# Attention stage of a decoder step on one core: where one block of maxima, the head loads and the page groups stand in a hand-written order

## The chip, the cores and the metric

The kernel runs on one core of one Trainium2 chip. The metric is device microseconds of a whole execution, the median of a few runs. The kernel before took 3463.64 us (three runs, 3452.68 to 3472.67). The core has a matrix engine (PE, TensorE; its weight loads are listed as PEld), a vector engine (DVE), a scalar engine (ACT), a general engine (POOL) and a sequencer that here only issues transfers (SP). Each works through its own instructions in program order and waits on semaphores for the others.

## The reference, cut to what matters

The program is one inference step of a two-layer decoder for a prompt of 2048 tokens and 8 samples of one token each. The change touches only the attention of layer 1, over 16 heads of 64 features:

```python
# prompt: every head, causal, with a cumulative forget bias ck
s = einsum('bqhd,bkhd->bhqk', q_i, k) * ATTN_SCALE + cq_i[..., :, None] - ck[:, :, None, :]
p = softmax(where(key_pos <= q_pos, s, -inf));  out = einsum('bhqk,bkhd->bqhd', p, v)
# samples: 8 of them, each over 32 cached pages of 128 rows (4096 keys) and its new row
past_v = cache_v[page_table].reshape(Bs, -1, C_HEADS, C_HEAD_DIM)
s = einsum('bqhd,bkhd->bhqk', q, k_all) * ATTN_SCALE + cq[..., :, None] - ck[:, :, None, :]
out = einsum('bhqk,bkhd->bqhd', softmax(where(mask, s, -inf)), v_all)
```

Everything is float32; the softmax needs the maximum of each query's row, or any value near it.

## The kernel before

The attention stage is one function, `attention`. The prompt's work is cut into units: unit u is head u // 4 and a block of 512 queries, u % 4. A unit has 4, 8, 12 or 16 *score steps*, one for each 128 keys that its queries may see, so a head has 40 steps and the stage 640. In the last four steps of a unit (the diagonal) the width shrinks from 512 queries to 384, 256 and 128, and a 128-wide matmul adds the causal mask.

A step n is, in the names of `schedule()`:

- QK: two matmuls into one of two PSUM tiles `at_st` (L2052, L2054, and the mask L2056). PE waits until the exponential of step n-2 is done. ACT then takes the exponential into one of six tiles `at_w` (L2121), and POOL adds it to the row sums `at_acc` (L1995).
- M: one block of maxima for a later unit. A matmul into one of two tiles `at_mx` (L2030, mask L2033), which DVE reduces (L2153). The two tiles are a ring: PE waits for the reduction of the block two before. When a unit's last block is reduced, MN takes its maximum (L2159), MR turns it into a row with four small matmuls (L2040), and ACT writes it as an extra row of the queries (L2138).
- PV: for every pair of steps, two matmuls of values with weights, side by side on the two halves of the array (L2069). OE and OF (ACT L2128, DVE L2168 and L2171) add the halves of a finished unit and apply the gate.
- LS: once for each head, the row sums (L2077), which are stored by L1874.

There are 640 blocks of maxima as well. Twelve are made before step 0. After that the number in a step is set by `pace`, which divides the blocks owed by the steps left, for units up to u+2: two a step in the first eight steps of a head, one a step in the next twenty-four, none in the last eight.

The sample attention is threaded through this. Each of the 8 samples gets 80 steps, two heads. Its ten small operations are SD, SM, SA, SB, SC, SS, SE, SL, SX and SR: decayed scores, their maximum over pages and partitions, exponential, sum, inverse. They go from DVE (SD, SM, SB, SS, SL, SR) to PE (SA, SC, SX) and ACT (SE) and back, each waiting for the one before. Then come eight page groups (VG 0 to 7, 16 matmul records each at L2101), the new row (VN), VM (DVE), VA (PE) and VC (DVE). `side` spreads these 22 evenly, one every 3.6 steps: SD at step 3, SR at 36, VG 0 at 39, then 43, 47, 50, 54, 58, 61 and 65, VN at 69.

All transfers are issued by SP in the order of the same list. A page group is four transfers of 512 KB into one of two buffers `at_vp` (L1878, function `values`); group r+2 is asked for when group r is used up. A head needs eight loads (LD, L1856), seven of them 512 KB, and its values (LV, L1861). LV fetches 2048 rows of 256 bytes. In `schedule` LD x of head h+1 stands at step 2+x of head h (for h from 1), and LV at step 10. Head 0 and head 1 are loaded before the first step; PE's first block of maxima waits for all eight loads of its head.

## Time and profile before

| what | value |
|---|---|
| median of three runs | 3463.64 us (3452.68 to 3472.67) |
| the profiled execution, its own time | 3444.23 us |
| its span, first to last instruction | 3442.6 us |
| mean granted clock of PE over the span | 0.927 of 2.4 GHz |
| first and last block of maxima's matmul in the attention stage (L2030) | 1956.7 and 3166.4 us |
| first and last score exponential (L2121) | 1970.8 and 3196.6 us |

The chain that ended last names only the last stage (`o_...`), 7% of the span, so it doesn't tell of attention. The stage must be read from its own windows. A stage in which PE is busy nearly all the time and idles in a few long gaps has its time in PE's work, in PE's clock and in those gaps. The window view gives, for each stretch, the busy time of each engine with its number of instructions, the granted clock of PE as a share of full speed, the busy share of the 16 DMA engines and their rate.

### The profile page before, as it was taken

What the parts mean: (1) busy time and instruction counts of PE and PEld (TensorE: products, weight loads), DVE (VectorE), ACT (ScalarE), POOL (GpSimd) and SP (SyncE); (2) the same over time, 40 slices, a digit from 0 to 9 for tenths busy, and PEclk for the clock granted to TensorE, in tenths of its full rate; (3) what the DMA queues carried; (4) which work ended last, traced back from release to release, by engine and by line L of the source; (5) the groups of instructions that cost most, each with busy time, mean ns of one, the idle gap of its engine ahead of it and who ended that gap; (6) DMA issues with size and microseconds to landing.
All of it is one profiled execution on the core that took longest, in us unless ns stands there. A gap on an engine that the chain in (4) does not pass through costs nothing. (4 is left out here: it accounts for less than half of the span.)

```text
span 3442.6 us, 46928 instructions
## 1 busy us (share of the span) xinstructions
PE 2965.1 (86%) x17133; PEld 2233.3 (65%) x17133; DVE 1591.6 (46%) x2148; ACT 1028.9 (30%) x1721; POOL 1377.1 (40%) x986
## 2 busy tenths in 40 slices
PE   3869797959889998889999398887989898899899
PEld 3869696947659998789999244443535344444687
DVE  5142323243556788865554453443435353444332
ACT  5222222231452221211121043433434343434200
POOL 0000000010003777678888264554657464556100
PEclk9989898979999999999999598998999898999899
DMA  3101010026545888788776557566574857664442
GB/s 114 32 23 41 32 37 25 24 83 182 170 144 170 268 278 273 250 288 255 245 254 223 138 148 219 143 188 178 143 208 126 248 136 217 156 193 161 151 129 69
DMA packets 327904, 547.51 MB, mean 159 GB/s; under 512 B 76093, under 2 KB 220129, under 8 KB 319212
## 3 DMA queue, kind: packets, MB, share of 16 engines
q1 hardware_dynamic: 263564, 471.12, 46.9%
q10 hardware_dynamic: 61120, 58.83, 4.9%
q0 software_dynamic: 3008, 14.81, 1.2%
q8 instruction: 124, 2.03, 0.2%
q14 instruction: 88, 0.72, 0.1%
HBM read 449.58 MB, written 95.12 MB: 158 GB/s over the span
## 5 line engine op out<-in xcount | busy, mean ns | idle before, releaser
L1995 POOL TENSOR_TENSOR at_acc<-at_acc,at_w 128x512 f32<-128x512 f32 (+3 forms) x576 | 640.1, 1111 | 420.1 <-ACT at_w L2121 370.6
L1151 POOL TENSOR_TENSOR p_kp<-p_kp,p_qb 128x1024 f32<-128x1024 f32 x256 | 628.6, 2484 | 388.8 <-DMA p_kp<-in_cache_k_dram 307.8
L2153 DVE TENSOR_REDUCE at_mx<-at_mx 128x1 f32<-128x512 f32 (+3 forms) x640 | 377.0, 608 | 642.4 <-PE at_mx L2030 369.9
L112 PE MATMUL p_pb<-p_w,x_xh 128*128 128x256 f32 x2048 | 592.3, 289 | 9.3 <-DVE p_w L1465 9.3
L2121 ACT ACTIVATE at_w<-at_st,c_nckt 128x512 f32<-128x512 f32 (+3 forms) x640 | 393.5, 623 | 672.1 <-PE at_st L2054 426.0
L113 PE MATMUL p_pb<-p_w,x_xh 128*128 128x256 f32 x2048 | 579.6, 283 | 0.0
L114 PE MATMUL p_pb<-p_w,x_xl 128*128 128x256 f32 x2048 | 579.3, 283 | 0.0
L1567 DVE TENSOR_REDUCE p_sc<-p_kp 128x16 f32<-128x1024 f32 x256 | 307.7, 1215 | 225.4 <-POOL p_kp L1151 225.3
L112 PEld LDWEIGHTS p_pb<-p_w,x_xh 128*128 128x128 f32 x2048 | 391.2, 191 | 21.6 <-issue 11.4
L113 PEld LDWEIGHTS p_pb<-p_w,x_xh 128*128 128x128 f32 x2048 | 392.5, 192 | 0.0
L114 PEld LDWEIGHTS p_pb<-p_w,x_xl 128*128 128x128 f32 x2048 | 391.8, 191 | 0.0
L112 PE MATMUL l_pb<-x_xh,l_wh 128*128 128x412 f32 x800 | 288.9, 361 | 73.5 <-DVE l_wl L857 73.5
L2069 PE MATMUL at_o<-at_w,at_v 128*64 128x512 f32 (+3 forms) x1280 | 335.3, 582 | 0.0
L2052 PEld LDWEIGHTS at_st<-at_q,at_k 128*128 128x128 f32 x640 | 125.3, 196 | 302.0 <-issue 148.4
L2030 PE MATMUL at_mx<-at_km,at_q 65*128 65x512 f32 (+3 forms) x640 | 253.8, 419 | 46.0 <-DMA at_k<-kl 22.1
L2052 PE MATMUL at_st<-at_q,at_k 128*128 128x512 f32 (+3 forms) x640 | 289.9, 453 | 0.0
L113 PE MATMUL l_pb<-x_xl,l_wh 128*128 128x412 f32 x800 | 286.1, 358 | 0.0
L114 PE MATMUL l_pb<-x_xh,l_wl 128*128 128x412 f32 x800 | 285.7, 357 | 0.0
L112 PE MATMUL o_pp<-o_wh,o_mh 128*128 128x512 f32 (+1 forms) x544 | 219.7, 404 | 36.8 <-DVE o_wl L586 22.4
L2101 PE MATMUL at_cv<-at_vp,at_sw 128*32 128x512 f32 x1056 | 164.1, 704 | 95.6 <-DMA at_vp<-in_cache_v_dram 95.6
L2054 PE MATMUL at_st<-at_q,at_k 65*128 65x512 f32 (+3 forms) x640 | 243.0, 380 | 0.0
L113 PE MATMUL o_pp<-o_wl,o_mh 128*128 128x512 f32 (+1 forms) x544 | 214.8, 395 | 0.0
(293 smaller groups left out, 3897.4 us busy)
## 6 DMA issues: line engine op xcount, KB each, us to landing
p_kp<-in_cache_k_dram SPq DMA_DIRECT2D x256, 512.0 KB, 4.8
at_vp<-in_cache_v_dram SPq DMA_DIRECT2D x256, 512.0 KB, 5.6
o_mt<-mixed SPq DMA_DIRECT2D x32, 512.0 KB, 5.6
p_raw<-in_w_in_dram SPq DMA_DIRECT2D x32, 512.0 KB, 7.0
at_q<-qh SPq DMA_DIRECT2D x32, 512.0 KB
at_k<-kh SPq DMA_DIRECT2D x32, 512.0 KB
l_raw<-in_w_in_dram SPq DMA_DIRECT2D x20, 512.0 KB
mixed<-l_w POOLq DMA_DIRECT2D x8, 1028.0 KB, 4.2
```

The costliest lines, as they stand in the source:

```text
L112: nc.tensor.matmul(out, lhs[0], rhs[0], start=(k == 0), stop=False)
L113: nc.tensor.matmul(out, lhs[0], rhs[1], start=False, stop=False)
L114: return nc.tensor.matmul(out, lhs[1], rhs[0], start=False, stop=(k == nk - 1))
L1151: nc.gpsimd.tensor_tensor(kp[:, g % 4], kp[:, g % 4], qb[:], ALU.mult).then_inc(kmul, 1)
L1567: nc.vector.tensor_reduce(sc[:, b % 2].rearrange("p (h g) -> p h g", g=z.PG)[:, :, r], by_head(kp[:, g % 4], z.H), AX.X, ALU.add).then_inc ...
L1995: nc.gpsimd.tensor_tensor(t[:, 512 - wd:512], t[:, 512 - wd:512], W[n % RW][:, 0:wd], ALU.add).then_inc(accd, 1)
L2030: last = nc.tensor.matmul(MX[r % 2][:, 0:wd], Q2[s][0:HR, t * P:(t + 1) * P], KM[s][0:HR, seg * 512:seg * 512 + wd], start=True, stop=seg < c)
L2052: nc.tensor.matmul(ST[n % 2][:, 0:wd], K1[s][:, ks], Q1[s][:, q0:q0 + wd], start=True, stop=False)
L2054: last = nc.tensor.matmul(ST[n % 2][:, 0:wd], K2[s][:, ks], Q2[s][:, q0:q0 + wd], start=False, stop=not diagonal)
L2069: last = nc.tensor.matmul(O[u % 2][HD * x:HD * x + HD, 512 - wd:512], V[s][:, kb + x, :], W[(n + x) % RW][:, 0:wd], start=kb == 0, stop=kb ...
L2121: nc.scalar.activation(W[n % RW][:, 0:wd], ST[n % 2][:, 0:wd], ACT.Exp, bias=C.nckt[:, kb, u // NC:u // NC + 1]).then_inc(ex, 1)
L2153: nc.vector.reduce_max(mx[:, u % 2, j, seg:seg + 1], MX[r % 2][:, 0:wd], AX.X).then_inc(mread, 1)
```

## The change

It sets the order by other rules, and gives the steps these places (counted from the start of a head for LD and LV, of a sample for the rest):

- M: up to two a step as long as fewer than n + 21 are done. In the first head that gives two a step for eight steps; after that it is exactly one in every step until all are done, 21 steps before the end.
- The ten small sample operations stand at steps 1 to 10, one a step. VG r stands at step 13 + 8r (13 to 69), VN at 71, VM 72, VA 74, VC 76.
- LD 0 to 7 stand at steps 2, 4, 4, 8, 14, 18, 22 and 26, LV at 11. Head 1 is loaded in the same way and no longer before the first step. A second semaphore (`ldm`) counts the three loads that the maxima need; the other five are waited for by the head's first score step.
- LS stands three steps earlier. There are six tiles `at_acc`, in turn by unit, in place of eight.
- PV is written so that it could take other than even pairs. With the pairs that the list has, its matmuls are the same as before.

```diff
@@ -1679,6 +1679,8 @@
     NLD = 8
     VG = PG // 4
     RW = 6
+    LEAD = 20
+    NA = 6
 
     def blocks(u):
         return 4 * (u % NC + 1)
@@ -1700,13 +1702,18 @@
         todo = [(v, j, seg) for v in range(U) for j in range(4) for seg in range(v % NC + 1)]
         tail = [("SD",), ("SM",), ("SA",), ("SB",), ("SC",), ("SS",), ("SE",), ("SL",), ("SX",), ("SR",)] \
             + [("VG", r) for r in range(VG)] + [("VN",), ("VM",), ("VA",), ("VC",)]
-        side = [(*w, b) for b in range(B) for w in tail]
+        at = [1 + x for x in range(len(tail) - VG - 4)] + [13 + 8 * r for r in range(VG)] + [71, 72, 74, 76]
+        span = N // B
+        side = {}
+        for b in range(B):
+            for w, x in zip(tail, at):
+                side.setdefault(span * b + x, []).append((*w, b))
         loads = {}
-        for h in range(2, H):
-            start = first_step(NC * (h - 1)) + 2
-            for x in range(NLD):
-                loads.setdefault(start + x, []).append(("LD", h, x))
-            loads.setdefault(start + NLD, []).append(("LV", h))
+        for h in range(1, H):
+            start = first_step(NC * (h - 1))
+            for x, later in enumerate((2, 4, 4, 8, 14, 18, 22, 26)):
+                loads.setdefault(start + later, []).append(("LD", h, x))
+            loads.setdefault(start + 11, []).append(("LV", h))
         later = {}
         seq, done, ring, turn_at, pending = [], 0, 0, {}, []
 
@@ -1752,14 +1759,7 @@
                     else:
                         seq.append(w)
                 seq.append(("QK", u, kb, n))
-                pace = 0
-                for v in range(u + 1, min(u + 3, U)):
-                    owed = sum(blocks(x) for x in range(0, v + 1)) - done
-                    left = first_step(v) - 4 - n
-                    pace = max(pace, -(-owed // left) if left > 0 else owed)
-                for _ in range(pace):
-                    if done == len(todo) or todo[done][0] > u + 2:
-                        break
+                for _ in range(min(2, min(len(todo), n + 1 + LEAD) - done)):
                     v = maximum()
                     if v is not None:
                         turn_at.setdefault(n + 2, []).append(v)
@@ -1771,9 +1771,8 @@
                     if p[1] == blocks(p[0]) - 2:
                         later.setdefault(n + 2, []).append(("OF", p[0]))
                         if p[0] % NC == NC - 1:
-                            later.setdefault(n + 8, []).append(("LS", p[0] // NC))
-                a0, a1 = (len(side) * n) // N, (len(side) * (n + 1)) // N
-                seq += side[a0:a1]
+                            later.setdefault(n + 5, []).append(("LS", p[0] // NC))
+                seq += side.pop(n, [])
                 n += 1
         for n in sorted(later):
             seq += later[n]
@@ -1781,7 +1780,7 @@
             weigh(p)
         seq.append(("OF", U - 1))
         sums(H - 1)
-        assert n == N and done == len(todo) and not turn_at and not loads
+        assert n == N and done == len(todo) and not turn_at and not loads and not side
         return seq
 
     SEQ = schedule()
@@ -1797,7 +1796,7 @@
         V = [S.sb(f"v_{s}", [P, z.NT, HD]) for s in range(2)]
         SG = [S.sb(f"sg_{s}", [HD, 512]) for s in range(2)]
         W = [S.sb(f"w_{x}", [P, 512]) for x in range(RW)]
-        acc = [S.sb(f"acc_{x}", [P, 512]) for x in range(2 * NC)]
+        acc = [S.sb(f"acc_{x}", [P, 512]) for x in range(NA)]
         ot = [S.sb(f"ot_{x}", [HD, 512]) for x in range(2)]
         og = [S.sb(f"og_{x}", [HD, 512]) for x in range(2)]
         lt = S.sb("lt", [P, 512])
@@ -1836,6 +1835,7 @@
             "table_in vnew_in scores_in new_scores_in new_scores_zeroed decayed smax sall ssub sexp ssum sl4 slsum srcp vpages vmasked"
             " vatt vcopied made masked sgs_in final fstored sl1 rl_bounded masks_rounded sdiag sspread smhd")
         ld = S.sems("head_in0 head_in1")
+        ldm = S.sems("head_for_max0 head_for_max1")
         sg_in = S.sems("gate_in0 gate_in1")
         val_in = S.sems("values_in0 values_in1")
         ogst = S.sems("out_stored0 out_stored1")
@@ -1853,7 +1853,7 @@
                 dst, src = ((Q2[s][0:HD], D.qh[hs, :]), (KM[s][0:HD], D.kh[hs, :]), (KM[s][HD:HR], D.nck[ds(h, 1), :]),
                             (K1[s][0:HD], D.kh[hs, :]), (K1[s][HD:P], D.kh[hs, :]), (Q1[s][0:HD], D.qh[hs, :]),
                             (Q1[s][HD:P], D.ql[hs, :]), (K2[s][0:HD], D.kl[hs, :]))[x]
-                sp.dma_start(dst.bitcast(F32), src).then_inc(ld[s], 16)
+                sp.dma_start(dst.bitcast(F32), src).then_inc((ldm if x < 3 else ld)[s], 16)
 
             def value_load(h):
                 if h >= 2:
@@ -1903,12 +1903,9 @@
             scores(0)
             sp.wait_ge(snz, 1)
             sp.dma_start(sn[0:1], D.snew.rearrange("(o b) h -> o b h", o=1)).then_inc(sn_in, 16)
-            for x in range(NLD):
-                head_load(1, x)
             sp.wait_ge(pt_in, 16)
             value_group(0, 0)
             value_group(0, 1)
-            value_load(1)
             for b in range(B):
                 sp.dma_start(sgs[:, :, b], D.sgs[b].rearrange("(k p) -> p k", p=P)).then_inc(sgs_in, 16)
             due = []
@@ -1984,17 +1981,17 @@
                     _, u, kb, n = w
                     h, c = u // NC, u % NC
                     wd = width(n)
-                    t = acc[NC * (h % 2) + c]
+                    t = acc[u % NA]
                     pool.wait_ge(ex, n + 1)
                     if kb == 0:
-                        if h >= 2:
-                            pool.wait_ge(lsm, h - 1)
+                        if u >= NA:
+                            pool.wait_ge(lsm, (u - NA) // NC + 1)
                         nc.gpsimd.tensor_copy(t[:], W[n % RW][:]).then_inc(accd, 1)
                     else:
                         pool.wait_ge(accd, n)
                         nc.gpsimd.tensor_tensor(t[:, 512 - wd:512], t[:, 512 - wd:512], W[n % RW][:, 0:wd], ALU.add).then_inc(accd, 1)
                     added = n + 1
-                elif w[0] == "LD" and w[2] == 0:
+                elif w[0] == "LD" and w[2] == 0 and w[1] >= 2:
                     h = w[1]
                     pool.wait_ge(qk, first_step(NC * (h - 1)))
                     pool.wait_ge(accd, added)
@@ -2022,7 +2019,7 @@
                     c, h = u % NC, u // NC
                     s = h % 2
                     if j == 0 and seg == 0 and c == 0:
-                        pe.wait_ge(ld[s], 16 * NLD * (h // 2 + 1))
+                        pe.wait_ge(ldm[s], 16 * 3 * (h // 2 + 1))
                         pe.wait_ge(onesd, max(2, h + 1))
                     ring_free(r)
                     t = 4 * c + j
@@ -2048,6 +2045,8 @@
                         pe.wait_ge(ex, n - 1)
                     if kb == 0:
                         pe.wait_ge(rowd, u + 1)
+                        if c == 0:
+                            pe.wait_ge(ld[s], 16 * (NLD - 3) * (u // NC // 2 + 1))
                     ks = slice(kb * P, (kb + 1) * P)
                     nc.tensor.matmul(ST[n % 2][:, 0:wd], K1[s][:, ks], Q1[s][:, q0:q0 + wd], start=True, stop=False)
                     diagonal = kb >= 4 * c
@@ -2065,16 +2064,16 @@
                     if kb == 0 and u >= 2:
                         pe.wait_ge(osum, u - 1)
                     for x in range(2):
-                        wd = width(n + x)
-                        last = nc.tensor.matmul(O[u % 2][HD * x:HD * x + HD, 512 - wd:512], V[s][:, kb + x, :], W[(n + x) % RW][:, 0:wd],
-                                                start=kb == 0, stop=kb == blocks(u) - 2)
+                        wd, y = width(n + x), HD * (x % 2)
+                        last = nc.tensor.matmul(O[u % 2][y:y + HD, 512 - wd:512], V[s][:, kb + x, :], W[(n + x) % RW][:, 0:wd],
+                                                start=kb + x < 2, stop=kb + x >= blocks(u) - 2)
                     last.then_inc(pv, 1)
                 elif w[0] == "LS":
                     _, h, r = w
                     pe.wait_ge(accd, HB * (h + 1))
                     ring_free(r)
                     for c in range(NC):
-                        last = nc.tensor.matmul(MX[r % 2][32 * c:32 * c + 32, :], ones32[:], acc[NC * (h % 2) + c][:], start=True, stop=True)
+                        last = nc.tensor.matmul(MX[r % 2][32 * c:32 * c + 32, :], ones32[:], acc[(NC * h + c) % NA][:], start=True, stop=True)
                     last.then_inc(lsm, 1)
                 elif w[0] == "SA":
                     pe.wait_ge(smaxd, w[-1] + 1)
```

PE, at the last steps of head 0 and the first of head 1, before (`at_st` are scores, `at_mx` on the left is a block of maxima, `at_o` values with weights, `at_cv<-at_vp` a page group):

```order
L2052 MATMUL at_st<-at_q_0,at_k_0 128x512
L2054 MATMUL at_st<-at_q_0,at_k_0 128x512
L2052 MATMUL at_st<-at_q_0,at_k_0 128x512
L2054 MATMUL at_st<-at_q_0,at_k_0 128x512
L2069 MATMUL at_o<-at_w,at_v 64x512 x2
...
L2101 MATMUL at_cv<-at_vp,at_sw 32x512 x8
L2052 MATMUL at_st<-at_q_1,at_k_1 128x512
L2054 MATMUL at_st<-at_q_1,at_k_1 128x512
L2056 MATMUL at_st<-at_identr,at_maskr 128x128
L2030 MATMUL at_mx<-at_km,at_q_1 128x512 x2
```

The same place now:

```order
L2051 MATMUL at_st<-at_q_0,at_k_0 128x512
L2053 MATMUL at_st<-at_q_0,at_k_0 128x512
L2027 MATMUL at_mx<-at_km,at_q_1 128x128
L2030 MATMUL at_mx<-at_maskr,at_identr 128x128
L2051 MATMUL at_st<-at_q_0,at_k_0 128x512
L2053 MATMUL at_st<-at_q_0,at_k_0 128x512
L2027 MATMUL at_mx<-at_km,at_q_1 128x512
L2068 MATMUL at_o<-at_w,at_v 64x512 x2
...
L2051 MATMUL at_st<-at_q_1,at_k_1 128x512
L2053 MATMUL at_st<-at_q_1,at_k_1 128x512
L2055 MATMUL at_st<-at_identr,at_maskr 128x128
L2027 MATMUL at_mx<-at_km,at_q_1 128x384
```

Steps 34 and 35 had no block of maxima and now have one each; step 40, the first of the next head, had two and now has one; and the page group at the head's last step is gone from there.

SP, at the loads of head 2 in the middle of sample 0, before (`at_q_0`, `at_km`, `at_k_0` are the head's loads, `at_v` its values, `at_vp` pages, `lsum` the store of the sums):

```order
L1856 DMA at_km<-nck 1x2048
L1870 DMA att<-at_og 64x512
L1865 DMA at_sg<-sg 64x512
L1856 DMA at_k_0<-kh 64x2048 x2
L1856 DMA at_q_0<-qh 64x2048
...
L1856 DMA at_q_0<-ql 64x2048
L1870 DMA att<-at_og 64x512
L1865 DMA at_sg<-sg 64x512
L1856 DMA at_k_0<-kl 64x2048
L1861 DMA at_v<-out_v_prompt_dram 128x16x64
L1874 DMA lsum<-at_lt 4x512
```

The same loads now:

```order
L1874 DMA lsum<-at_lt 4x512
L1856 DMA at_k_0<-kh 64x2048
L1870 DMA att<-at_og 64x512
L1865 DMA at_sg<-sg 64x512
L1861 DMA at_v<-out_v_prompt_dram 128x16x64
...
L1856 DMA at_k_0<-kh 64x2048
L1870 DMA att<-at_og 64x512
L1865 DMA at_sg<-sg 64x512
L1856 DMA at_q_0<-qh 64x2048
```

The store of the sums, which stood right behind the values' load, stands ahead of it, and a page group (the rows left out, four transfers) and two units' stores now stand between loads that were issued one after the other.

## Rows read from the trace of the kernel before

**Rows 1.** The page: the span.

```profile
span 3442.6 us, 46928 instructions
```

**Rows 2.** What PE waited for, 1950 to 3200 us: total, times, longest.

```profile
PE at_cv L2101 <- DMA at_vp<-in_cache_v_dram: 95.6, 17, 11.0
...
PE at_mx L2030 <- DVE at_mx L2153: 19.8, 46, 1.3
```

**Rows 3.** Windows, one for each sample's 80 steps (first, last, sum of eight).

```profile
core 0: us, PE busy (x) PEld busy (x) DVE busy (x) ACT busy (x) POOL busy (x), PEclk, DMA share, GB/s
1970.83:2126.58 155.75, 139.15 (x652) 70.46 (x652) 65.03 (x116) 59.55 (x97) 86.54 (x81) 0.88 0.67 189
...
3064.36:3196.99 132.63, 128.45 (x633) 62.40 (x633) 59.38 (x104) 58.90 (x97) 85.27 (x80) 0.96 0.49 142
sum 1226.16, PE 1098.01 PEld 539.48 DVE 524.62 ACT 483.10 POOL 703.15; mean PE 137.25 PEld 67.43 DVE 65.58 ACT 60.39 POOL 87.89
```

**Rows 4.** Windows of sample 5: steps 0-12, 12-24, 24-32, 32-40, 40-52, 52-64, 64-72, 72-80.

```profile
2756.96:2778.50 21.54, 19.93 (x95) 10.51 (x95) 15.46 (x29) 9.24 (x17) 12.97 (x14) 1.00 0.78 175
2778.50:2796.14 17.64, 16.37 (x77) 8.96 (x76) 11.13 (x19) 8.80 (x15) 13.27 (x12) 1.00 0.43 80
2796.14:2806.68 10.54, 10.54 (x51) 6.07 (x50) 8.12 (x13) 7.64 (x12) 7.37 (x7) 1.00 0.13 26
2806.68:2817.47 10.79, 10.79 (x59) 4.84 (x58) 0.32 (x2) 5.12 (x9) 9.79 (x8) 1.00 0.00 0
2817.47:2844.03 26.56, 25.25 (x142) 11.80 (x142) 14.29 (x26) 9.23 (x16) 14.17 (x16) 1.00 0.96 264
2844.03:2881.57 37.54, 25.82 (x123) 10.82 (x122) 9.31 (x16) 8.80 (x15) 12.98 (x12) 0.77 0.93 284
2881.57:2895.82 14.25, 14.25 (x70) 6.62 (x69) 7.13 (x12) 6.68 (x11) 8.99 (x8) 1.00 0.55 179
2895.82:2909.48 13.66, 13.66 (x58) 7.34 (x56) 0.58 (x2) 5.34 (x9) 9.33 (x9) 0.75 0.53 181
```

**Rows 5.** Windows of the last sample: steps 52-64 and 72-80.

```profile
3154.43:3174.88 20.45, 20.45 (x115) 8.93 (x114) 7.20 (x11) 8.69 (x15) 13.03 (x12) 1.00 0.96 334
...
3186.67:3196.99 10.32, 10.32 (x49) 5.64 (x48) 0.17 (x1) 4.54 (x8) 8.82 (x8) 0.83 0.01 2
```

**Rows 6.** Windows of steps 52-64, samples 0 to 6: their sum.

```profile
sum 272.40, PE 182.32 PEld 76.19 DVE 65.15 ACT 61.57 POOL 90.77; mean PE 26.05 PEld 10.88 DVE 9.31 ACT 8.80 POOL 12.97
```

**Rows 7.** Timeline of SP in sample 5: start, duration, instruction.

```profile
2842.10 0.59 SPq L1861 DMA_DIRECT2D at_v<-out_v_prompt_dram  x1
2842.74 14.54 SPq L1874 DMA_DIRECT2D lsum<-at_lt  x1
```

**Rows 8.** Timeline of PE in sample 5, page group 4.

```profile
2853.84 3.64 PE L2101 MATMUL at_cv<-at_vp,at_sw 128*32 128x512 f32 x16 [7.43 <-DMA at_vp<-in_cache_v_dram]
```

**Rows 9.** Windows, the last sample's steps 52-64, page matmuls alone.

```profile
3154.43:3174.88 20.45, 5.77 (x48) 1.25 (x48) 1.00 0.96 334
```

**Rows 10.** Groups by form, 1950 to 3200 us: DVE, ACT and POOL.

```profile
L2153 DVE TENSOR_REDUCE at_mx<-at_mx 128x1 f32<-128x512 f32 x448 | 302.8, 688 | 444.7 <-PE at_mx L2030 369.9 <-PE at_mx L2033 72.1
...
L2194 DVE TENSOR_REDUCE at_l<-at_sw 128x32 f32<-128x1056 f32 x8 | 16.5, 2065 | 0.0
...
L2141 ACT ACTIVATE at_sw<-at_sd 128x528 f32<-128x528 f32 x8 | 9.3, 1166 | 0.0
...
L1995 POOL TENSOR_TENSOR at_acc<-at_acc,at_w 128x512 f32<-128x512 f32 x384 | 496.0, 1292 | 336.0 <-ACT at_w L2121 304.0
```

**Rows 11.** Timeline of the stage's beginning: POOL, PE.

```profile
1946.30 0.34 POOL L1970 MEMSET at_onesh<- 16x128 f32 x1
...
1956.65 0.44 PE L2030 MATMUL at_mx<-at_km,at_q 65*128 65x128 f32 x1 [22.05 <-DMA at_k<-kl]
...
1968.55 0.77 PE L2052 MATMUL at_st<-at_q,at_k 128*128 128x512 f32 x1
```

## The prediction

> **What bounds the kernel now.** I read the page first: its chain covers the last 7% of the span alone, so attention has to be read from windows. The waits of PE over the stage come next [rows 2]. One wait stands out: 95.6 us in 17 waits, up to 11.0 us long, for a page group from memory. Waits for DVE's reductions of the maxima, the ring of two tiles, add up to only 19.8 us. The windows per sample [rows 3] show PE busy for 1098.01 of 1226.16 us while DVE, ACT and POOL are each busy for 703 us or less: PE sets the pace, by its work, its clock and its gaps. The first and the last sample, and what the sum leaves for the rest, show the next thing. The last takes 132.63 us and the other seven (1226.16 - 132.63) / 7 = 156.2 us each, with nearly the same work. The last is the one with no further head to load. It also lacks the final 20 blocks of maxima, which I price below.
>
> The windows within one sample say where the difference is. Steps 52 to 64 take 37.54 us in sample 5 at a clock of 0.77 [rows 4], 272.40 / 7 = 38.9 us on average [rows 6], and 20.45 us at full clock in the last [rows 5], with the same three page groups. So it is not the page traffic alone that is late there: the last sample draws its pages at 334 GB/s without a wait. It is the head's loads, all at steps 42 to 50 between page groups 1 and 4. SP's own timeline shows how this hurts [rows 7]: after the values' load it is held for 14.54 us at issuing the next transfer, 8 KB of row sums, and what stands behind it, the request for page group 5, goes out only after that. PE waits 7.43 us for group 4 and then takes 3.64 us for it [rows 8]; in the last sample a group costs 5.77 / 3 = 1.92 us [rows 9]. That is the other half of the loss: after the gap PE runs at 1.2 instead of 2.4 GHz for a while.
>
> Meanwhile steps 24 to 40 of the same sample move next to nothing, 26 and 0 GB/s [rows 4]. The memory traffic is bunched; it isn't too much.
>
> **Term 1, the page groups spread (VG every 8 steps, loads spread too).** After the change a group comes every 8 steps and is asked for 16 steps ahead. At the 1.3 to 1.5 us a step of the undisturbed windows (10.54 / 8, 17.64 / 12, [rows 4]) plus a quarter microsecond a step for the groups, 16 steps are about 25 us. Demand: a sample draws 176 GB/s or so over some 155 us, the 173 to 189 of its windows, so about 28 MB (189 x 155.75 = 29.4 MB in the first [rows 3], the last, with fewer loads, 142 x 132.63 = 18.8 MB). In 130 us that is 215 GB/s, against 334 GB/s that the queue has shown [rows 5] and 264 to 284 while it was crowded [rows 4]. So I take the waits to be gone, and the clock with them. Price: steps 52 to 64 fall from 38.9 to the last sample's 20.45 plus four blocks of maxima that it lacked, at 0.25 us, 21.5 us: 17.4 us in each of seven samples, 122 us. A few samples also lose some time in steps 44 to 52, which I put at 9 us together. Term 1: -131 us. If nothing is gained (the wait only moves), it is 0; more than the whole difference to the last sample, 7 x (156.2 - 132.6) = 165 us, it can't be.
>
> The groups themselves cost the same wherever they stand, 1.92 us each. VN, VM, VA and VC also only move.
>
> **Term 2, one block of maxima a step.** It moves eight blocks per head, from its first eight steps to the last eight of the head before. Before, steps 0 to 12 took 21.54 us [rows 4] with DVE busy 15.46 us, and steps 40 to 52 took 26.56, from which three groups (5.8) and LS (about 1) come off: 19.8. What do twelve such steps cost with one block each? The nearest row is steps 52 to 64 of the last sample without its groups, 20.45 - 5.8 = 14.7 us, with wider scores but only eight blocks; I take 15. That saves 6.5 and 4.8 us, 5.65 a head. On the other side the last eight steps of a head get eight blocks. Full-width steps with a block take 10.54 / 8 = 1.32 us; without one, and with a group, narrower steps take 10.79 [rows 4], 8.9 without the group, 1.1 each. So a block costs about 0.25 us, 2 us for eight. Head 0 stays as it was and gets only the extra; the last gets only the saving: 15 x 5.65 - 15 x 2 = 55 us. Term 2: -55 us; bounds -20 (if DVE was no part of it, and only PE's order changes) and -85 (if the added blocks hide in PE's waits for ACT).
>
> **Term 3, the ten small operations one a step.** This is what gets worse. PE takes three of them in order (SA, SC, SX) and stands still until DVE or ACT has delivered. In steps 1 to 10 DVE now has two units' OF, ten or eleven reductions of at most 0.69 us, and all of the sample's work, of which the sum over the weights alone is 2.07 us, and ACT's exponential of 1.17 us [rows 10] comes before that. SX at step 9 waits for both in a row: 3.2 us and the copy behind them, against two steps of PE. I price it at +3.5 us a sample, less about 1 us that such a stall cost before in steps 12 to 24 (17.64 us there [rows 4] against the 15.7 of rows 5 without groups, but with the blocks it lacked). Term 3: 8 x 2.5 = +20 us. Bounds: 0 and, if all of the chain were exposed (about 9 us a sample), +72 us. Behind a waiting SX stand the next scores, and behind these ACT and POOL; POOL's adds at 1.29 us each have room in a 1.5 us step, so nobody else becomes late.
>
> **Term 4, the clock outside of steps 40 to 64.** Steps 72 to 80 without any block took 13.66 us at a clock of 0.75 in sample 5, and 10.32 at 0.83 in the last [rows 4, 5]. With blocks in them PE is busier. I take 2 us a sample, -15 us in all; bounds 0 and -30.
>
> **Term 5, the beginning.** PE's first block stood until 1956.65 for the last of eight loads [rows 11]. It now waits for the first three. PE's other condition, constants of POOL, is met at 1946.6 [rows 11]. The first twelve blocks and two MR take 1956.65 to 1968.55, 11.9 us, and can now run before the other loads land. Score step 0 starts at about 1958.6: -10 us, bounds 0 and -12.
>
> LS three steps earlier: it has waited for POOL for almost nothing, and I price it at 0, at worst 1 us a head, +16. Six sum tiles instead of eight: the first that is reused is unit 6's, at step 52, long after LS. PV: no change.
>
> **The sum.** -131 - 55 + 20 - 15 - 10 = -191 us. The span of 3442.6 us [rows 1] becomes about 3252, and that execution's 3444 about 3253. It was a quick one: the median of the runs is 3464. Taking the same difference from the median gives 3273; I say 3270. As a check, eight samples of 80 steps by the windows at full clock: 15 + 3.5, then 15.7 + 3.8 (two groups), 10.5 + 1.9, 8.9 + 2 + 1.9, 15 + 1 + 1.9, 15.7 + 3.8, 14.2, and 10.3 + 2 make 127 us, 1016 in all, against 1226: -210, of which the first sample's slow beginning (about 13 us, two blocks a step at half clock) and some slow stretches come back.
>
> At one place a rule speaks against it. The values' load moves 2048 pieces of 256 bytes, and the row shows SP held for 14.54 us right behind it [rows 7]. The Trainium skill, DMA: Bandwidth & Descriptors, Specifications, says the same from the other side: below 512 B per piece a transfer doesn't reach the line rate. By that rule the load stays as costly as it was, and it now stands at step 11, two steps ahead of a page request.
>
> **Rivals.** A, the transfers stay late in part. For: the change puts the values' load at steps 11 and 51 of a sample, just ahead of the requests at VG 0 and VG 5, so SP may be held there twice. Against: the groups then asked for are needed 16 steps later, 25 us, more than the 14.54. If half of term 1 stays, -125 us: 3340.
>
> B, slower: the same mechanism at its full price. If SP is held behind both values' loads long enough that groups 2 and 7 land late, each place costs PE what one place costs now, 17.4 us a sample, in all 14 to 16 places: 15 x 17.4 = 261 us, against 131 now, so term 1 turns into +130, and with the others +70: 3534. It decides from about 25 us between request and landing; a hold of 14.54 plus a group in 8 leaves it just short. The rule above would have it, if small pieces were what fills the queue.
>
> C, the chain of small operations is exposed in full and PE's clock falls there as it did behind the page groups: term 3 at +72 and term 4 at 0, -124 us: 3340.
>
> D, the change does not do what it says: SP runs ahead of PE, so the spread exists only where SP waits (VG, stores). Then loads bunch again, between other groups. That is A's price. And the maxima are only moved for 8 of 40 steps, which term 2 already counts.
>
> **How the numbers follow.** The forecast has 0.70, A with D 0.13, C 0.12, B 0.04, and 0.01 for nothing measurable. Its own range is 3215 to 3310; over the cases, 3205 to 3345. A run-to-run difference of about 0.5% (17 us) is what can be told from no change: faster 0.95, same 0.01, slower 0.04.
>
> **What will show it.** In the profile after: PE's wait for page groups near 0 instead of 95.6 us; no window of 12 steps over 24 us after the first sample; the clock in steps 52 to 64 at 1.0; DMA at 150 GB/s or more in steps 24 to 40. The seven samples are at 127 to 131 us. In steps 0 to 12, 17 to 19 us, with short waits of PE for DVE at SA, SC and SX. PE's first block at 1947 and score step 0 at about 1959. It would be wrong if a page wait of several us stood behind step 29 or 69 (B), or if steps 0 to 12 took over 22 us (C).

## The result and the profile after

The changed kernel took 3315.81 us (median of four runs, 3305.91 to 3319.65) against 3468.15 us for the kernel before: a ratio of 0.9546, 95% interval 0.9475 to 0.9616. That is 4.5% less, 152 us by the medians. Between the two profiled executions it is 3442.6 - 3304.3 = 138 us of span. The forecast was 191 us. The time lies 6 us above the forecast's own range (3215 to 3310), and within the one over all its cases (3205 to 3345).

The page of the changed kernel, the span:

```profile
span 3304.3 us, 46930 instructions
```

What PE waited for in the attention stage (total, times, longest), to be read beside [rows 2]:

```profile
PE at_mx L2027 <- POOL at_onesh L1967: 12.2, 1, 12.2
PE at_mx L2037 <- DVE at_mneg L2158: 12.1, 16, 1.2
...
PE at_mx L2027 <- DVE at_mx L2152: 7.2, 9, 1.0
PE at_cv L2086 <- DVE at_l L2195: 7.0, 7, 1.3
PE at_cv L2080 <- DVE at_smx L2181: 2.5, 6, 0.5
```

The wait for page groups, 95.6 us before, is gone entirely. New are the waits of the small operations SX (L2086) and SA (L2080) for DVE, 9.5 us. MR's (L2037) is as long as before, when it was 9.6 + 2.0 us. The first block of maxima waited 22.1 us for the head's loads and now waits 12.2 us for POOL's constants.

Windows of the changed kernel, one for each sample's 80 steps, columns as in [rows 3] (first, fourth, last, sum):

```profile
1959.72:2101.38 141.66, 140.27 (x662) 74.11 (x662) 69.63 (x124) 60.03 (x97) 86.70 (x81) 0.88 0.81 223
...
2374.48:2511.34 136.86, 133.25 (x666) 67.73 (x666) 68.11 (x118) 61.22 (x99) 88.86 (x82) 0.94 0.72 202
...
2929.47:3057.31 127.84, 124.37 (x624) 61.67 (x623) 56.66 (x96) 59.25 (x97) 85.86 (x80) 0.95 0.49 143
sum 1097.59, PE 1070.95 PEld 546.17 DVE 534.72 ACT 486.63 POOL 705.66; mean PE 133.87 PEld 68.27 DVE 66.84 ACT 60.83 POOL 88.21
```

The samples add up to 1226.16 - 1097.59 = 129 us less. The first exponential is at 1959.72 instead of 1970.83 us, which is another 11; behind the attention 1.4 us are lost again. PE's idle time in the eight windows, their length less PE's busy time, falls from 1226.16 - 1098.01 = 128 us [rows 3] to 27 us. So about four fifths of what the samples won is idle time.

Windows of sample 3, the stretches of [rows 4]: steps 0-12, 12-24, 24-32, 32-40, 40-52, 52-64, 64-72, 72-80:

```profile
2374.48:2397.94 23.46, 20.21 (x89) 11.13 (x89) 16.31 (x28) 10.22 (x17) 12.97 (x13) 0.83 0.54 124
2397.94:2420.11 22.17, 22.17 (x107) 10.24 (x107) 9.13 (x16) 8.79 (x15) 13.26 (x12) 0.87 0.63 162
2420.11:2432.59 12.48, 12.48 (x65) 6.28 (x64) 6.38 (x11) 6.68 (x11) 9.04 (x8) 1.00 0.99 284
2432.59:2445.31 12.72, 12.72 (x68) 6.29 (x67) 4.73 (x8) 5.44 (x10) 9.34 (x9) 1.00 0.48 175
2445.31:2463.46 18.15, 17.79 (x100) 9.41 (x100) 10.18 (x18) 9.18 (x16) 12.51 (x13) 1.00 0.97 292
2463.46:2482.85 19.39, 19.39 (x107) 9.59 (x106) 9.13 (x16) 8.79 (x15) 13.43 (x13) 1.00 1.00 252
2482.85:2497.15 14.30, 14.30 (x69) 6.64 (x68) 6.39 (x11) 6.67 (x10) 9.78 (x8) 1.00 0.52 134
2497.15:2511.34 14.19, 14.19 (x68) 8.15 (x67) 5.85 (x10) 5.44 (x9) 8.53 (x8) 0.88 0.60 233
```

The forecast's check had 18.5, 19.5, 12.4, 12.8, 17.9, 19.5, 14.2 and 12.3 us for these. Five of the eight came within 0.3 us. Three did not: steps 0 to 12 (+5.0), 12 to 24 (+2.7) and 72 to 80 (+1.9), and these are the ones with a clock below 1.00. In this sample the miss is 9.5 us; over all eight it is 1097.59 - 1016 = 82 us, 10 a sample. That has to be explained. From the second sample on, steps 0 to 12 take between 22.50 and 25.58 us, so this sample is not an odd one.

The timeline of PE and DVE in the same sample, steps 7 to 10 (start, duration, instruction, idle time before it), shows where the clock falls in the first of them:

```profile
2385.77 1.08 PE L2068 MATMUL at_o<-at_w,at_v 128*64 128x512 f32 x4
...
2389.28 0.49 PE L2027 MATMUL at_mx<-at_km,at_q 65*128 65x512 f32 x1 [0.99 <-DVE at_mx L2152]
2389.70 1.65 PE L2068 MATMUL at_o<-at_w,at_v 128*64 128x512 f32 x4
2392.03 0.59 PE L2086 MATMUL at_cv<-c_onescol,at_l 128*128 128x1 f32 x2 [0.67 <-DVE at_l L2195]
...
2394.78 1.97 PE L2068 MATMUL at_o<-at_w,at_v 128*64 128x512 f32 x4
```

DVE at the same time:

```profile
2385.85 0.69 DVE L2189 TENSOR_TENSOR at_sd<-at_sd,at_cv 128x528 f32<-128x528 f32 x1
...
2387.24 1.78 DVE L2170 TENSOR_TENSOR at_og<-at_og,at_sg 64x512 f32<-64x512 f32 x1
2388.95 0.87 DVE L2152 TENSOR_REDUCE at_mx<-at_mx 128x1 f32<-128x128 f32 x2
2389.75 1.94 DVE L2193 TENSOR_REDUCE at_l<-at_sw 128x32 f32<-128x1056 f32 x1
2391.72 0.25 DVE L2195 COPY at_l<-at_l 128x96 f32<-128x96 f32 x1
```

DVE has SS (L2189), a unit's OF (L2170) and the sum over the weights (SL, L2193) behind one another. PE waits twice, under 1 us each. But the values' matmuls behind that take 1.65 and 1.97 us instead of 1.08: the granted clock is 0.50 from 2392 to 2402 us, which is 1.2 GHz, and the first page group, at 2400.58, still takes 3.46 us instead of 1.92. PE's waits for DVE listed above add up to 3.6 us a sample (28.8 / 8), but the kernel before had 3.9 ((19.8 + 9.6 + 2.0) / 8), so only the 9.5 / 8 = 1.2 us of SX and SA are new. The clock takes 2.7 us in steps 12 to 24 alone, and more ahead of them.

### The profile page after: what moved, and what is told of

Its sections match the earlier page's. It is cut to its first block and busy times, and to the rows that moved or that the text cites. A ratio compares the mean times of both kernels' runs of the same rounds, so it can differ in the third digit from the quotient of the medians.

```text
span 3304.3 us, 46930 instructions
## 1 busy us (share of the span) xinstructions
PE 2939.4 (89%) x17133; PEld 2242.9 (68%) x17133; DVE 1599.6 (48%) x2148; ACT 1032.1 (31%) x1721; POOL 1376.5 (42%) x986
## 5 line engine op out<-in xcount | busy, mean ns | idle before, releaser
L2068 PE MATMUL at_o<-at_w,at_v 128*64 128x512 f32 (+3 forms) x1280 | 342.9, 593 | 0.0
L2027 PE MATMUL at_mx<-at_km,at_q 65*128 65x512 f32 (+3 forms) x640 | 266.8, 420 | 19.7 <-POOL at_onesh L1967 12.2
L114 PE MATMUL o_pp<-o_wh,o_ml 128*128 128x512 f32 (+1 forms) x544 | 215.1, 395 | 0.0
```

The source lines that it names most:

```text
L114: return nc.tensor.matmul(out, lhs[1], rhs[0], start=False, stop=(k == nk - 1))
L2027: last = nc.tensor.matmul(MX[r % 2][:, 0:wd], Q2[s][0:HR, t * P:(t + 1) * P], KM[s][0:HR, seg * 512:seg * 512 + wd], start=True, stop=seg < c)
L2068: last = nc.tensor.matmul(O[u % 2][y:y + HD, 512 - wd:512], V[s][:, kb + x, :], W[(n + x) % RW][:, 0:wd], start=kb + x < 2, stop=kb + x >= ...
```

## The experiments

Eleven kernels ran, each beside the kernel before on the same chip. Ratios are to that kernel, with their 95% interval. The changed kernel ran at another time than numbers 4 to 10, and the medians of the kernel before beside them all lie between 3465.65 and 3471.49 us; so differences between two edited kernels are good to a few us only. Each kernel has one profiled execution, which need not be its median one.

**1. Loads alone, on the kernel before (b_loads).**

```diff
-        for h in range(2, H):
-            start = first_step(NC * (h - 1)) + 2
-            for x in range(NLD):
-                loads.setdefault(start + x, []).append(("LD", h, x))
-            loads.setdefault(start + NLD, []).append(("LV", h))
+        for h in range(1, H):
+            start = first_step(NC * (h - 1))
+            for x, later in enumerate((2, 4, 4, 8, 14, 18, 22, 26)):
+                loads.setdefault(start + later, []).append(("LD", h, x))
+            loads.setdefault(start + 11, []).append(("LV", h))
...
+        ldm = S.sems("head_for_max0 head_for_max1")
```

> The kernel before with the loads alone moved (LD at steps 2, 4, 4, 8, 14, 18, 22, 26, LV at 11, head 1 loaded during head 0, two semaphores for a head's loads); page groups, small operations and maxima as before. Theory P (the groups' bunching, one every 3.6 steps, is what makes them late; the loads only add to it): the groups still ask for 16 MB within 26 steps, some waits stay, PE's wait for pages falls from 95.6 us to 30 to 60, and with the 10 us of the earlier beginning the kernel is 50 to 80 us faster. Theory L (the head's loads and the values' load ahead of a page request make them late): PE's wait for pages falls under 10 us, steps 52 to 64 take 22 us instead of 39, and the kernel is about 140 us faster.

Measured: 3431.6 us, 0.9866 (0.9824 to 0.9908). PE's wait for pages in it:

```profile
PE at_cv L2101 <- DMA at_vp<-in_cache_v_dram: 56.0, 20, 6.4
```

So spreading the loads takes 40 of 95.6 us of waits, as theory P had it. The time falls by 34 us by the medians, less than P's 50 to 80, and about 10 us of it are the earlier beginning. The sum of the profiled execution's eight windows, to be read beside [rows 3], shows where the rest may go:

```profile
sum 1229.69, PE 1141.12 PEld 560.61 DVE 526.49 ACT 482.72 POOL 701.15; mean PE 142.64 PEld 70.08 DVE 65.81 ACT 60.34 POOL 87.64
```

PE idles 89 us instead of 128, but is busy for 43 us more with the same work, at a clock of 0.82 to 0.94 in the windows. (It was the slowest of the four runs.) One more thing shows here and in numbers 3 and 11, whose page groups stand at the old places too: all waits for pages fall in the first seven samples. The last, with its groups as close together but no further head to load, has none.

**2. Sample work alone (b_pages).** Page groups every 8 steps and the small operations at 1 to 10, with the old loads and maxima.

```diff
+        at = [1 + x for x in range(len(tail) - VG - 4)] + [13 + 8 * r for r in range(VG)] + [71, 72, 74, 76]
...
-                a0, a1 = (len(side) * n) // N, (len(side) * (n + 1)) // N
-                seq += side[a0:a1]
+                seq += side.pop(n, [])
```

> The kernel before with the sample's side work alone moved (ten small operations at steps 1 to 10, page groups every 8 steps from 13, VN 71, VM 72, VA 74, VC 76); loads and maxima as before. Theory P: PE's wait for pages is gone (under 10 us), page term -130 us. Theory L: the loads at steps 42 to 50 and the 14.5 us hold of the transfer issuer stay, so about half of the wait stays, 30 to 50 us. In both, the small operations meet steps with two blocks of maxima each: steps 0 to 12 take 25 to 30 us instead of 21.5, +30 to +60 us over the kernel. Sum by P -70 to -100 us, by L 0 to -50 us.

Measured: 3330.3 us, 0.9616 (0.9566 to 0.9666): 135 us faster, nearly all of the change's gain and more than either theory had. PE's waits for pages are zero, although SP is still held behind the values' load, for up to 14.44 us once the first sample is over. Its steps 0 to 12, in sample 4:

```profile
2522.55:2544.84 22.29, 20.47 (x99) 11.02 (x99) 18.73 (x36) 10.26 (x17) 12.78 (x13) 1.00 0.82 187
```

22.29 us, against 21.54 in [rows 4], each at full clock. Only two of the eight samples here ran these steps at full clock; the other six took 24.31 to 25.22 us at 0.77 to 0.86. But the kernel before has such samples too: the average of the eight is 24.30 us here, 23.52 before and 24.52 in the changed kernel. So where the steps are long anyway for their two blocks of maxima, the chain of small operations adds under 1 us; both theories had put these steps at 25 to 30 us.

**3. Maxima alone (b_maxima).**

```diff
-                pace = 0
...
-                for _ in range(pace):
-                    if done == len(todo) or todo[done][0] > u + 2:
-                        break
+                for _ in range(min(2, min(len(todo), n + 1 + LEAD) - done)):
```

> The kernel before with the order of the maxima alone changed to one block a step, 20 ahead. By the prediction's term 2: -55 us, with steps 0 to 12 at 16 to 18 us instead of 21.5 and steps 32 to 40 at 12.8 instead of 10.8. Page waits stay at 80 to 96 us. Rival: the eight steps without maxima were a pause that let DVE and the page traffic catch up, and the blocks just move: within 10 us of the kernel before, steps 72 to 80 as much longer as steps 0 to 12 are shorter.

Measured: 3485.03 us, 1.0045 (1.0009 to 1.0081): slower, if anything, by 19 us, where term 2 had 55 us faster and the rival within 10. Windows of its sample 3, steps 0-12, 12-24 and 40-52:

```profile
2471.84:2489.51 17.67, 16.71 (x85) 8.95 (x85) 11.74 (x21) 9.19 (x16) 13.02 (x13) 1.00 0.80 174
2489.51:2511.74 22.23, 20.96 (x77) 11.05 (x76) 11.14 (x19) 8.80 (x15) 13.22 (x12) 0.77 0.45 90
...
2535.03:2563.93 28.90, 23.82 (x132) 10.38 (x132) 10.38 (x18) 9.19 (x17) 12.76 (x13) 0.94 0.97 253
```

And PE's wait for pages in the same kernel:

```profile
PE at_cv L2095 <- DMA at_vp<-in_cache_v_dram: 107.6, 23, 8.7
```

The sum of its eight windows:

```profile
sum 1265.36, PE 1146.68 PEld 571.35 DVE 534.36 ACT 486.58 POOL 704.03; mean PE 143.34 PEld 71.42 DVE 66.79 ACT 60.82 POOL 88.00
```

Steps 0 to 12 did fall from 21.54 to 17.67 us, in three samples; in the other five they took 20.23 to 29.57 at a lower clock. In this sample steps 12 to 24 ran at a clock of 0.77, 22.23 us instead of 17.64. Its steps 40 to 52 take 28.90 instead of 26.56, and the last eight steps of each head carry 2 us more. Waits for pages rise by 12 us, but PE's idle time as a whole doesn't: it is 119 us against 128 before. What the order gives, PE's clock takes: PE is busy for 1146.68 us against 1098.01. Why the clock falls more often here is open.

**4. Small operations at every second step, on the changed kernel (a_chain2).**

```diff
-        at = [1 + x for x in range(len(tail) - VG - 4)] + [13 + 8 * r for r in range(VG)] + [71, 72, 74, 76]
+        at = [1 + 2 * x for x in range(len(tail) - VG - 4)] + [20 + 7 * r for r in range(VG)] + [71, 72, 74, 76]
```

> The changed kernel with the ten small operations at every second step (1, 3, ... 19) and the page groups at 20 + 7r; all else as changed. Theory C (PE stands still behind the chain of small operations at steps 1 to 10, and its clock falls to 1.2 GHz for what follows): steps 0 to 24 take 36 to 38 us a sample instead of 40 to 41 (17.5 and 19.5 us), the half clock at steps 10 to 14 is gone, 30 to 40 us faster than the changed kernel. Rival N (the narrow diagonal steps are themselves too thin for PE's clock, whatever stands between them): within 8 us of the changed kernel.

Measured: 3273.39 us, 0.9408 (0.9366 to 0.9451), 42 us below the changed kernel. Theory C holds: steps 12 to 24 take 18.27 us at full clock in every sample. Steps 0 to 12 take 19.54 to 20.93 from the second sample on, still at a clock of 0.77 to 0.91. The edit also moves the page groups, the first from step 13 to 20; that was not tried apart, but the clock in the timeline above fell ahead of step 13.

**5. The old maxima in the changed kernel (a_pace).** The reverse of the edit in 3.

> The changed kernel with the maxima by the old rule (two blocks in each of a head's first eight steps, none in its last eight); page groups, small operations and loads as changed. Theory S (the chain of small operations makes steps 0 to 12 about 22 us long whether PE has one or two blocks a step in them, so moving the blocks saves nothing there and adds 2 us to the last eight steps): within 15 us of the changed kernel, steps 0 to 12 at 22 us, 32 to 40 at 10.7 instead of 12.7. By the prediction's term 2 it would be 55 us slower than the changed kernel.

Measured: 3326.51 us, 0.9583 (0.9525 to 0.9641). That is 11 us above the changed kernel, with intervals that overlap: in this surrounding, the maxima's new order is worth little or nothing by the medians. The profiled execution differs by more. The sum of its windows:

```profile
sum 1134.33, PE 1109.24 PEld 561.55 DVE 516.15 ACT 484.11 POOL 703.24; mean PE 138.66 PEld 70.19 DVE 64.52 ACT 60.51 POOL 87.90
```

That is 37 us above the changed kernel's 1097.59; it was the slowest of its four runs, and the changed kernel's the quickest. Theory S holds for the time, but its reason doesn't: it had steps 0 to 12 at 22 us with one block or two, and they took 28.58 us on average (in sample 2, 31.40 at a clock of 0.60), against 24.52 in the changed kernel.

**6. The old loads in the changed kernel (a_oldloads).** The reverse of the edit in 1.

> The changed kernel with the loads at their old places (LD at steps 2 to 9, LV at 10, head 1 before the first step, PE's first block waits for all eight). With the page groups spread, the loads have room wherever they stand: page waits stay under 5 us, and only the beginning is lost, 5 to 10 us slower than the changed kernel. Rival: the loads' bunching needs the spreading too, page waits of 20 us or more, 30 us or more slower.

Measured: 3358.31 us, 0.9699 (0.9627 to 0.977), 42 us above the changed kernel. Expected were 5 to 10. The rival was nearer in size, but with another wait: none for pages, though SP is held for up to 12.6 us behind the values' load once the first sample is over, and

```profile
PE at_mx L2029 <- DMA at_k<-kl: 49.4, 8, 22.2
```

22.2 us of it is the beginning as before. The other seven, 3.9 us each, are the first block of maxima for an even head, at step 60, which asks for all eight loads of that head; steps 52 to 64 take 23.5 to 27.6 us instead of 19.4. In b_pages the same loads were in time, since its steps 40 to 52 are 4.7 us longer (22.80 against 18.15). So loads and maxima belong together: the quicker the steps, the earlier the loads are wanted. Whether the spread or the second semaphore does it was not tried apart.

**7. VA in four pieces, on the changed kernel (a_va4).**

```diff
-            + [("VG", r) for r in range(VG)] + [("VN",), ("VM",), ("VA",), ("VC",)]
+            + [("VG", r) for r in range(VG)] + [("VN",), ("VM",)] + [("VA", x) for x in range(4)] + [("VC",)]
...
-                    for k in range(z.KB):
+                    for k in (2 * w[1], 2 * w[1] + 1):
```

> The changed kernel with VA (8 products of 128x128 weights with one column, 16 matmul records, 1.9 us in one piece at step 74) cut into four pieces of two products at steps 74 to 77, VC at 78. Theory V (the one piece in which PE has weights to load but only one column each to stream is what takes its clock to 1.2 GHz at step 75 or 76 in every sample): no half clock in steps 72 to 80, these take 12.5 us instead of 14.2 to 18.8, 15 to 35 us faster than the changed kernel. Rival: the clock falls by itself in the narrow steps 76 to 79: no difference.

Measured: 3263.43 us, 0.9395 (0.9336 to 0.9454). In every sample steps 72 to 80 are at full clock:

```profile
2500.16:2512.82 12.66, 12.66 (x68) 7.66 (x67) 5.94 (x10) 5.45 (x9) 8.56 (x8) 1.00 0.68 257
```

The same matmuls took 14.19 us at 0.88 in the changed kernel, and 18.44 in its sample 5. Over the eight samples these steps give 21 us, within the 15 to 35 expected. The medians differ by 52 us, more than that and more than the profiled executions show (3304.3 and 3288.4 us of span); a_va4's four runs lie between 3252.76 and 3289.98. How the rest arises is open: its steps 4 to 24 still had low-clock stretches of changing length.

How sure is it that VA does it? In the nine kernels with VA in one piece the clock fell within 4 us behind it in 44 of 72 samples: in all eight of the changed kernel, but in only three of number 6. In the four kernels with VA in pieces (numbers 7 to 10) it fell in none of 32, up to the end of the attention's last step. So one piece makes the fall possible, not certain.

**8. Both (a_chain2_va4).**

> Both: small operations at every second step, groups at 20 + 7r, and VA in four pieces. If the two costs are separate, 42 us (measured for the first) and 15 to 35 us for the second add up: 60 to 75 us faster than the changed kernel, at 3240 to 3255 us, steps 0 to 24 at 35 us a sample at full clock. If the clock just falls at the next thin place instead (steps 0 to 4 or 76 to 80), the second adds under 10 us.

Measured: 3236.87 us (3236.17 to 3244.43), 0.9335 (0.9278 to 0.9392), 79 us below the changed kernel and the fastest of all. The two costs alone, 42 and 52 us, add up to more, and 60 to 75 had been expected. Windows of it, samples 0 and 3, and the sum:

```profile
1959.14:2095.81 136.67, 134.65 (x662) 71.03 (x662) 70.15 (x124) 60.02 (x98) 86.83 (x81) 0.92 0.82 231
...
2352.96:2481.49 128.53, 126.35 (x666) 65.07 (x666) 67.74 (x118) 61.16 (x99) 89.18 (x82) 1.00 0.77 215
...
sum 1029.05, PE 1011.80 PEld 520.56 DVE 532.69 ACT 486.30 POOL 707.80; mean PE 126.48 PEld 65.07 DVE 66.59 ACT 60.79 POOL 88.47
```

Steps 0 to 12 and 12 to 24 of sample 3:

```profile
2352.96:2370.97 18.01, 16.85 (x87) 9.27 (x87) 13.48 (x24) 9.18 (x16) 13.11 (x13) 1.00 0.69 163
2370.97:2389.25 18.28, 17.80 (x93) 9.42 (x92) 11.12 (x20) 9.72 (x15) 13.35 (x12) 1.00 0.48 123
```

From the second sample on no window's clock is below 1.00, and six samples take 128.5 us each. That is the forecast's 127 us within 1.5. Its arithmetic for a sample at full clock was right; what it missed was what takes the clock away.

**9. The old maxima here (c_pace).** The edit of 5 on the kernel of 8.

> The kernel with small operations at every second step and VA in four pieces (128.5 us a sample, no half clock from the second sample on), but the maxima by the old rule. Here nothing else makes steps 0 to 12 long, so the term for the maxima should show: steps 0 to 12 at 21 to 22 us instead of 18, 40 to 52 at 22.5 instead of 20.6, 32 to 40 and 72 to 80 shorter by 2 each. By the windows +1.5 to +3 us a sample, 12 to 25 us slower; by the prediction's term 2, 55 us slower. If PE's clock falls again in the steps with two blocks, in which it waits for the ring, it is 40 us or more.

Measured: 3270.58 us, 0.9421 (0.9366 to 0.9476), 34 us above number 8, where 12 to 25 had been expected. The two intervals touch, but the runs don't: 3259.53 is its quickest and 3244.43 the slowest of number 8. Steps 0 to 12 of its sample 3:

```profile
2366.04:2387.73 21.69, 20.25 (x97) 10.86 (x97) 16.66 (x32) 9.26 (x17) 12.75 (x13) 1.00 0.65 147
```

3.7 us a sample (132.25 against 128.53), the rest mostly from samples with low-clock stretches. In this undisturbed sample steps 0 to 12 are 3.7 us longer than in number 8 and steps 40 to 52 4.1 (24.65 against 20.54), while steps 32 to 40 and 72 to 80 are 2.0 shorter each. Here the maxima's order is worth 34 us; the forecast had 55.

**10. Small operations every third step, groups every six (c_chain3).**

```diff
-        at = [1 + 2 * x for x in range(10)] + [20 + 7 * r for r in range(VG)] + [71, 72, 74, 75, 76, 77, 78]
+        at = [1 + 3 * x for x in range(10)] + [29 + 6 * r for r in range(VG)] + [72, 73, 74, 75, 76, 77, 78]
```

> The same kernel (maxima one a step, VA in four pieces) with the small operations at every third step (1, 4, ... 28) and the page groups every 6 steps from 29 to 71. Theory 1: at every second step the chain still costs a little, about 1 us a sample in steps 4 to 24, so this is up to 10 us faster. Theory 2: it costs nothing any more, and groups every 6 steps, 2 MB in about 10 us or 200 GB/s beside the head loads, bring back some page waits: same or up to 20 us slower.

Measured: 3258.76 us, 0.9405 (0.9349 to 0.9462), 22 us above number 8, by theory 2:

```profile
PE at_cv L2100 <- DMA at_vp<-in_cache_v_dram: 13.0, 7, 4.0
```

With 6 steps to a group the pages are late again. The one sample before the last without such a wait takes 128.31 us, as in number 8: spreading the chain further gives nothing more.

**11. The values' load alone moved behind the page groups (b_values).**

```diff
-            loads.setdefault(start + NLD, []).append(("LV", h))
+            loads.setdefault(start + 22, []).append(("LV", h))
```

> The kernel before with one thing moved: the values' load LV stands at step 24 of the head instead of 10, behind the page groups instead of among them. Theory H (the 14.5 us for which the transfer issuer is held behind the values' load make group 5 late): PE's wait for pages falls from 95.6 us to 50 or less, 40 to 70 us faster. Theory Q (the queue is full there whatever stands in it: 16 MB of pages and 3.7 MB of loads within 26 steps): the wait falls by less than a third, under 30 us faster.

Measured: 3444.5 us, 0.9942 (0.9909 to 0.9974). The profiled execution was the quickest of its ten runs.

```profile
PE at_cv L2101 <- DMA at_vp<-in_cache_v_dram: 53.7, 14, 10.8
```

The wait falls by 42 us, the time by 25. SP is no longer held: between 1990 and 3060 us no request takes over 1.3 us. Both theories are half right: without the hold, part of the wait goes, as H had it, but over half stays. Nor are 16 MB of pages within 26 steps too much by themselves, for the last sample draws them without a wait [rows 5]; it takes the pages close together and a head's loads among them. The time gains less than the wait, as low-clock stretches remain; its sample 5 took 157.1 us.

## Why the prediction was right or wrong

**What bounds the kernel** was read rightly in kind: PE, with page waits and the clock behind them. The weight was wrong in one point: the prediction laid the late groups on the head's loads and on SP's hold of 14.54 us behind the values' load. Spreading the groups alone ended the waits (number 2), spreading the loads alone ended 40 of 95.6 us (1), and moving the values' load ended 42 (11). With the groups close together and no loads, in the last sample, there is no wait either. So it takes both, and taking the groups apart is the surest cure. The hold alone does not make pages late: it stays, at 10 to 14 us in every second head, in numbers 2 and 6, which have no page waits, and it is gone in number 11, which has 53.7 us of them. The prediction's own row says so too: the 7.43 us of [rows 8] are a wait for group 4, and the last request ahead of the hold, at 2836.02 us, was already that group's.

**Term 1** (-131): the seven windows of steps 52 to 64 fell from 272.40 us [rows 6] to 7 x 19.39 = 136 us, which is 137, and the one long stretch in steps 44 to 52 went as well. One of the three page groups there now stands elsewhere, so about 13 us of the 137 is work that moved. The term holds in size. Steps 24 to 40 now carry 284 and 175 GB/s.

**Term 2** (-55) is a step that failed, by its surroundings. It compared windows at full clock in which nothing but the maxima bounded the steps. Alone on the kernel before, the edit gained nothing and cost 0.45% (3), with PE's clock lower and its idle time no longer. In the changed kernel it is worth 11 us by the medians (5). Only with chain and VA spread does it bring 34 us (9). Even with the clock at 1.00 it is 3.7 us a sample and not the 7.3 of the forecast. One reason shows in the windows: terms 2 and 3 were added as if they stood apart, but with two blocks of maxima the chain adds next to nothing to steps 0 to 12 (21.69 us in number 9 against 21.54 before), and with one block it does (18.01 us in number 8, against the 15 taken for a stretch without it). How much of the loss in the changed kernel is this and how much the clock stays open.

**Term 3** (+20) was sized too small, and this is the largest part of the miss. 42 us come back when the chain is spread over twice the steps (4). I had priced PE's stalls, 2.5 us a sample, but not the clock that they take from the steps right behind them. Steps 0 to 12 and 12 to 24 together took 7.6 us more than forecast in sample 3, and 7.1 on average from the second sample on. Rival C named this mechanism, at 9 us a sample or +72. By the medians it is 20 + 42 = 62; by the windows, 2.5 + 7.1 = 9.6 us a sample, it came in full. The prediction's sign of C, steps 0 to 12 over 22 us, showed in every sample.

**Term 4** (-15) had the wrong sign: I expected the added maxima to hold the clock up in steps 72 to 80. It fell there in each sample, to 0.88 and below, and not for lack of maxima: VA cut in four ends it (7). These steps took 14.84 us on average against 12.3 in the forecast. I had costed VA as a piece that only moves.

**Term 5** (-10) was right: PE's first block at 1945.5, score step 0 at 1957.4, 11.1 us sooner, of which 9.8 are the shorter wait (12.24 instead of 22.05 us). PE waits for LS's sums for 0.2 us in all. Six sum tiles and PV were not tried apart.

**Rivals A and B** did not come. The issuer is still held behind the values' load at times (7.09 us for the four pages at 2330.85, of which 3.6 is usual), and a group asked for 16 steps ahead covers that. The rule that pieces below 512 B don't reach the line rate (the Trainium skill, DMA: Bandwidth & Descriptors, Specifications) pointed at the transfer behind which SP is held. No run here measures that transfer's rate, and no time hung on the hold: number 8, the fastest kernel, is held there for up to 9.49 us in every second head and has no page wait.

**The sum**: the check by windows at full clock had 210 us less, the windows gave 129, and the 82 between them are the low-clock stretches of steps 0 to 24 and 72 to 80 in the main. That the time still fell within the range over all cases is owed to rivals A and C at 3340, which widened it: 3316 us lies nearer to C's time than to the forecast's 3270. Of the prediction's other signs, the end of the page waits and the clock and traffic of the middle steps came; samples of 127 to 131 us did not (136.20 to 141.10 for the second to seventh).

## What to carry to other kernels

Before adding up terms, ask for each whether another one bounds the same stretch: the maxima's new order was worth -19, 11 or 34 us, by what stood beside it. Spread the transfers too: with the loads at their old places the quicker steps wanted them too early (number 6). Read idle time and busy time apart, since a lower clock can eat what shorter waits give (number 1). And count, for every small chain or odd piece of matrix work, not its own stall alone but the clock of the several us that come after it.

## What the runs showed of the hardware

PE's clock went to 1.2 GHz without a wait of PE. Around VA in the changed kernel:

```profile
2361.66 1.08 PE L2068 MATMUL at_o<-at_w,at_v 128*64 128x512 f32 x4
...
2363.42 1.89 PE L2107 MATMUL at_cv<-c_onescol,at_cm 128*128 128x1 f32 x16
...
2366.04 1.88 PE L2068 MATMUL at_o<-at_w,at_v 128*64 128x512 f32 x4
```

PE is listed as busy throughout; the granted clock is 1.00 over VA and 0.66 from 2365.31 to 2368.00 us. The 16 matmuls of VA load 128 columns of weights each and stream one column, and the same four matmuls of values take 1.08 us ahead of them and 1.88 us behind. With the 16 spread over four steps the clock stays. A busy PE is thus not always one that keeps its clock, though it did so behind the same 16 in 28 of 72 samples.

A transfer of 2048 pieces of 256 bytes held the issuer for 14.54 us at the next transfer when 3.7 MB of other loads stood before it [rows 7]; without it the same loads held nothing (number 11). With the loads spread, no transfer in the changed kernel's attention was held for more than 3.8 us once the first sample was under way; in number 8, where a head's load comes next instead of a page, it was up to 9.49 us.

The kernel before lay between 3442 and 3506 us over its 33 runs beside these, and number 8, with its clock at 1.00 from the second sample on, within 8 us in four. That the spread goes with the clock is likely but not shown by so few.
